# A mixture-of-experts stage of a two-block transformer: hidden activations turned on VectorE, slot tokens gathered with fp32r products, final rows fetched by indirect DMA

## The reference, cut to what matters

```python
logits = (hf @ router_w + router_b).astype(jnp.float32)
top_logit, top_idx = lax.top_k(logits, TOP_K)                 # TOP_K = 4, 256 tokens
gates = jax.nn.softmax(top_logit, axis=-1)
...
def expert_block(args):
    xb, e = args
    y = clamped_swiglu(xb @ w_gu[e] + b_gu[e])                # 1024 -> 2 * 1024, then 1024
    return y @ w_down[e] + b_down[e]
...
y_rows = y_rows * row_gate[:, None].astype(y_rows.dtype)
out = jax.ops.segment_sum(y_rows, row_tok, num_segments=n_tok + 1)[:n_tok]
...
x = x + g2 * moe_ffn(...)
return rmsnorm(x, final_g)
```

## Time and profile before

| | us |
|---|---|
| median of three runs | 3607.09 |
| lowest and highest of the runs | 3606.88, 3608.83 |
| the profiled execution, span of its instructions | 3608.5 |
| TensorE busy | 3112.7 (86%) |
| VectorE, ScalarE, GpSimd busy | 1452.6, 898.5, 298.1 |

### The profile page before, as it was taken

One profiled execution on the slowest core, in us unless ns is written; L12 is line 12 of the kernel. 1 busy time (PEld: TensorE's weight loads), 2 busy tenths in 40 slices (PEclk: granted clock), 3 DMA queues, 4 the chain that ended last, 5 costly groups with the idle time before them and its releaser, 6 DMA issues. The chain is left out here.

```text
span 3608.5 us, 95079 instructions
## 1 busy us (share of the span) xinstructions
PE 3112.7 (86%) x42406; PEld 2242.3 (62%) x42406; DVE 1452.6 (40%) x2335; ACT 898.5 (25%) x1523; POOL 298.1 (8%) x236
## 2 busy tenths in 40 slices
PE   5978879998887888787897976676999999999996
PEld 3855558887565676674786866543566566666653
DVE  3355653333763554556565765524111111111111
ACT  2114322222223343332343542201011000111100
POOL 0021200000411132230000104000000000000000
PEclk7989889999898999997998987887999999999998
DMA  7242432222143101003653430222999999999993
GB/s 288 82 158 77 155 140 85 101 96 93 38 155 123 50 21 38 34 4 125 233 187 121 166 115 3 101 102 94 399 404 406 408 407 405 406 405 406 409 405 139
DMA packets 220724, 684.11 MB, mean 190 GB/s; under 512 B 26096, under 2 KB 51184, under 8 KB 187712
## 3 DMA queue, kind: packets, MB, share of 16 engines
q1 hardware_dynamic: 190288, 647.72, 46.8%
q10 hardware_dynamic: 30192, 32.77, 2.7%
HBM read 659.46 MB, written 20.97 MB: 189 GB/s over the span
## 5 line engine op out<-in xcount | busy, mean ns | idle before, releaser
L3480 PE MATMUL experts_psum_gu<-ring,experts_x 128*32 128x256 f32 x9216 | 507.9, 381 | 16.6 <-ACT experts_x L3524 16.6
L3480 PEld LDWEIGHTS experts_psum_gu<-ring,experts_x 128*32 128x32 f32 x9216 | 295.6, 110 | 219.8 <-ACT experts_x L3524 16.9
L3584 DVE TENSOR_TENSOR experts_gate<-experts_psum_gu,experts_bias 128x768 f32<-128x768 f32 x32 | 30.6, 957 | 864.4 <-PE experts_psum_gu L3480 864.4
L3503 PE MATMUL experts_psum_down<-experts_weights,experts_hiddenT 128*32 128x256 f32 x6144 | 339.0, 380 | 4.3 <-ACT experts_hiddenT L3532 4.3
L3503 PEld LDWEIGHTS experts_psum_down<-experts_weights,experts_hiddenT 128*32 128x32 f32 x6144 | 199.5, 110 | 137.9 <-issue 6.3
L818 PE MATMUL mlp_psum_bank<-mlp_x_high,mlp_w_high 128*128 128x512 f32 (+1 forms) x512 | 174.8, 341 | 12.8 <-DVE xT_rounded L322 12.8
L3528 ACT ACTIVATE experts_sigmoid<-experts_gate 128x768 f32<-128x768 f32 x32 | 27.0, 843 | 615.5 <-DVE experts_gate L3586 615.5
L296 DVE TENSOR_TENSOR ring_rounded<-ring,mlp_w_high 128x1024 fp32r<-128x1024 f32 x128 | 156.7, 1225 | 51.3 <-ACT mlp_w_high L291 51.3
L818 PE MATMUL mlp_psum_bank<-xT_rounded,mlp_w_high 128*128 128x512 f32 (+1 forms) x512 | 175.4, 342 | 0.0
L818 PE MATMUL mlp_psum_bank<-mlp_x_high,ring_rounded 128*128 128x512 f32 (+1 forms) x512 | 173.6, 339 | 0.0
L3480 PE MATMUL experts_psum_gu<-xT,experts_x 128*32 128x256 f32 x3072 | 171.6, 379 | 0.0
(11 more groups left out here) (729 smaller groups left out, 5761.9 us busy)
## 6 DMA issues: line engine op xcount, KB each, us to landing
ring<-in_w_gu SPq DMA_DIRECT2D x186, 1024.0 KB, 18.9
experts_weights<-in_w_down SPq DMA_DIRECT2D x128, 1024.0 KB, 20.7
ring<-in_ada_w SPq DMA_DIRECT2D x36, 2048.0 KB, 9.0
ring<-in_mlp_w SPq DMA_DIRECT2D x32, 2048.0 KB, 7.9
xT<-in_w_gu SPq DMA_DIRECT2D x64, 1024.0 KB, 20.3
ring<-in_w_in SPq DMA_DIRECT2D x12, 2048.0 KB, 7.6
ring<-in_ab_w_in SPq DMA_DIRECT2D x6, 2048.0 KB, 9.1
ring<-in_w_rkv SPq DMA_DIRECT2D x6, 2048.0 KB, 8.4
```

Source lines behind the costliest of these rows:

```text
L3480: mm = nc.tensor.matmul(pg[o, q, gr, :], x, w[:, c:c + C], start=(u == 0 and gr != 1), stop=(u == U - 1), skip_group_check=True)
L3503: mm = nc.tensor.matmul(pd[o, gr, :], hidT[:, ch, gr, GROUP * v:GROUP * v + GROUP], w[:, ch, C * c:C * c + C], start=(v == 0 and ch == 0 a ...
L3584: v.tensor_tensor(gt[:, :, :], pg[:, 0, 0:GROUPS, :], rep(bias[:, 0, :], GROUPS), ALU.add).then_inc(s_bg, 1)
```

## The change

1. The loads of the router's weights and of the output biases move into norm2m's fetch.
2. In the router the tokens are split into a high part (rounded to fp32r) and a low part (the rest, rounded to fp32r; GpSimd subtracts). `S` is fp32r and lies in the memory of `acc`. The gather takes two single-pass products where one fp32 product stood, in groups of four PSUM banks: the half t = 0 of the group first, then t = 1. `s_S` is raised after each half of `S`. `gsel` is gone, and `rank` is copied to integers.
3. In the experts VectorE turns blocks of 32x32 of the hidden activations (`turned`) where TensorE and ScalarE turned blocks of 128x128; the rows of `w_down` are put in the order that this asks for. A wait for the last read of `gu` in PSUM (`s_bu`) goes ahead of `gate_up`.
4. In the last stage GpSimd fetches the four rows of each token by eight indirect DMAs of 128 rows (512 KB), and VectorE multiplies by the gates and sums. The table for the square root is loaded ahead, and the norm is done for each half apart.

```diff
@@ router @@
-        with nc.Block() as block:
-            @block.sync
-            def _(sync):
-                sync.dma_start(w[:, :, :], rw.rearrange("(a p) n -> p a n", p=P)).then_inc(s_ld, 16)
-                sync.dma_start(bd[:, :], bdown).then_inc(s_ld, 16)
...
-                pe.wait_ge(s_S, 1)
-                pe.wait_ge(s_tokc, 4)
-                for kt in range(KT):
-                    for sh in range(2):
-                        n = 2 * kt + sh
-                        if n >= 4:
-                            pe.wait_ge(s_xgc, n - 3)
-                        for t in range(2):
-                            mm = nc.tensor.matmul(pb[:, n % 4, :], htok[:, t, kt * P:(kt + 1) * P],
-                                                  S[:, t, sh * 512:(sh + 1) * 512], start=(t == 0), stop=(t == 1))
-                        mm.then_inc(s_xg, 1)
+                pe.wait_ge(s_high, 4)
+                pe.wait_ge(s_low, 4)
+                for first in range(0, 2 * KT, 4):
+                    for t in range(2):
+                        if first == 0:
+                            pe.wait_ge(s_S, t + 1)
+                        for n in range(first, first + 4):
+                            kt, sh = divmod(n, 2)
+                            if t == 0 and n >= 4:
+                                pe.wait_ge(s_xgc, n - 3)
+                            for q, h in enumerate((h_high, h_low)):
+                                mm = nc.tensor.matmul(pb[:, n % 4, :], h[:, t, kt * P:(kt + 1) * P],
+                                                      S[:, t, sh * 512:(sh + 1) * 512], start=(t + q == 0), stop=(t + q == 2))
+                            if t:
+                                mm.then_inc(s_xg, 1)
...
+                    nc.scalar.copy(h_high[:, n // 2, c], pb[:, n, :]).then_inc(s_high, 1)
+                    nc.scalar.copy(htok[:, n // 2, c], pb[:, n, :]).then_inc(s_tokc, 1)
...
+                    nc.gpsimd.tensor_tensor(h_low[:, n // 2, c], htok[:, n // 2, c], h_high[:, n // 2, c].bitcast(F32),
+                                            ALU.subtract).then_inc(s_low, 1)
@@ experts @@
                 def gate_up(i):
                     pe.wait_ge(s_x, i + 1)
+                    pe.wait_ge(s_bu, i + 1)
...
                 def down(i):
-                    pe.wait_ge(s_tc, i + 1)
+                    pe.wait_ge(s_t, i + 1)
                     pe.wait_ge(s_y, i + 1)
...
                 with pe.Fori(0, last) as i:
                     gate_up(i + 1)
                     down(i)
-                    turn_hidden(i + 1)
...
+                def turned():
+                    v.transpose(hidT[:, :, :, :].rearrange("p a b c -> p (a b c)"), up[:, :, :].rearrange("p a b -> p (a b)"))\
+                        .then_inc(s_t, 1)
+
+                v.sem_inc(s_bu, 1)
                 hidden(0)
+                turned()
                 with dve.Fori(0, last_item(dve)) as i:
                     hidden(i + 1)
+                    dve.wait_ge(s_dn_used, i * V + 2 * V)
+                    turned()
@@ final @@
+            @block.gpsimd
+            def _(pool):
+                for t in range(2):
+                    for k in range(TOP_K):
+                        nc.gpsimd.indirect_dma_start(yt[:, t, k, :], None, y_dram[0:N_PAIR, :],
+                                                     bass.IndirectOffsetOnAxis(rank_int[:, t, k:k + 1], 0))\
+                            .then_inc(s_yt[t][k], 16)
...
+                    for k in range(TOP_K):
+                        dve.wait_ge(s_yt[t][k], 16)
+                        ch.link(nc.vector.scalar_tensor_tensor(out=a, in0=yt[:, t, k, :], scalar=topg[:, t, k:k + 1], in1=a,
+                                                               op0=ALU.mult, op1=ALU.add))
                     ch.link(nc.vector.tensor_tensor(a, a, gate_row, ALU.mult))
                     nc.vector.tensor_tensor(g.x[:, 2 + t, :], g.x[:, 2 + t, :], a, ALU.add).then_inc(s_x, 1)
...
+                    if t:
+                        dve.wait_ge(s_row, 16)
+                        finish(dve, ch, 0)
+                finish(dve, ch, 1)
@@ the caller @@
             norm_T(g, "norm2m", LAT_TILES, g.xT, lambda t: mod(4, t), lambda t: mod(3, t), gains[:, 1, :], off=2,
-                   fetch=Fetch(g, "ldmoe", [(rb[:, :], row(a["router_b"])), (iota[:, :], row(a["iota"]))]))
+                   fetch=Fetch(g, "ldmoe", [(rb[:, :], row(a["router_b"])), (iota[:, :], row(a["iota"])),
+                                            (rw[:, :, :], a["router_w"].rearrange("(a p) n -> p a n", p=P)),
+                                            (bd[:, :], a["b_down"])]))
```

More of the change, by code:

```diff
@@ L3169, with router @@
 N_ITEM = N_EXP + (N_PAIR - 1) // (ITEM + 1) + 1
-def router(g, rw, rb, iota, bdown, acc, rank, topg, XgT, table, S, gsel):
+def router(g, w, rb, iota, bd, acc, rank, rank_int, topg, XgT, table, S):
     nc = g.nc
     with Phase(g, "router") as ph:
-        w = ph.sb("w", [P, KT, N_EXP])
-        bd = ph.sb("bd", [N_EXP, D])
         lg = ph.sb("logits", [P, 2, N_EXP])
@@ L3372, in _ @@
                     v.tensor_copy(gT[:, t, :], pl[0:N_EXP, t, 0:P]).then_inc(s_gc, 1)
-                for t in range(2):
-                    ch.link(v.tensor_scalar(gsel[:, t, :], iota, rank[:, t, 0:1], topg[:, t, 0:1],
-                                            ALU.is_equal, ALU.mult))
-                    for k in range(1, TOP_K):
-                        ch.link(v.tensor_scalar(g.tmp[:, :], iota, rank[:, t, k:k + 1], topg[:, t, k:k + 1],
-                                                ALU.is_equal, ALU.mult))
-                        ch.link(v.tensor_tensor(gsel[:, t, :], gsel[:, t, :], g.tmp[:, :], ALU.add))
                 ch.wait()
@@ L3409, in experts @@
         s_gt, s_up, s_pr, s_sg, s_h = (ph.sem(x) for x in ("gate", "up", "product", "sigmoid", "hidden"))
-        s_t, s_tc, s_y, s_st, s_end = (ph.sem(x) for x in ("turned", "turned_copied", "y", "stored", "end"))
+        s_t, s_y, s_st, s_end = (ph.sem(x) for x in ("turned", "y", "stored", "end"))
         def unit(u):
@@ L3566, in _ @@
                     result(i)
-                    turned(i + 1)
                 sigmoid(last)
                 result(last - 1)
-                turned(last)
                 result(last)
@@ L3896, in block2 @@
             norm_T(g, "norm2m", LAT_TILES, g.xT, lambda t: mod(4, t), lambda t: mod(3, t), gains[:, 1, :], off=2,
-                   fetch=Fetch(g, "ldmoe", [(rb[:, :], row(a["router_b"])), (iota[:, :], row(a["iota"]))]))
+                   fetch=Fetch(g, "ldmoe", [(rb[:, :], row(a["router_b"])), (iota[:, :], row(a["iota"])),
+                                            (rw[:, :, :], a["router_w"].rearrange("(a p) n -> p a n", p=P)),
+                                            (bd[:, :], a["b_down"])]))
             gate_rows(g, "rows3", [lambda kt: g.mods[0][:, 40 + kt, 0:1]], rows)
-            router(g, a["router_w"], rb[:, :], iota[:, :], a["b_down"], acc, rank[:, :, :], topg[:, :, :], XgT,
-                   table, acc, gsel)
+            router(g, rw, rb[:, :], iota[:, :], bd, acc, rank[:, :, :], rank_int[:, :, :], topg[:, :, :], XgT,
+                   table, slots)
         experts(g, a["w_gu"], a["w_down"], a["b_gu"], XgT, table, y_dram)
-        final(g, acc, gsel, y_dram, rows[:, 0, :], row(a["final_g"]), out)
+        final(g, acc, rank_int, topg, y_dram, rows[:, 0, :], row(a["final_g"]), out)
 def program(nc, a, out, parts=(0, 1, 2), x_out=None):
@@ L3958, in program, with hidden_order @@
         store(g, "stx", [(x_out[t], g.x[:, t, :]) for t in range(TT)])
+def hidden_order(w):
+    e, d, n = w.shape
+    return np.ascontiguousarray(w.reshape(e, 4, 8, 32, n).transpose(0, 2, 1, 3, 4).reshape(e, d, n))
 def layout(i):
```

117 lines of the change are left out of this document (43 added, 74 removed).

## The result

| | before | after |
|---|---|---|
| median of four runs, us | 3606.99 | 3552.04 |
| lowest and highest | 3606.74, 3608.83 | 3549.18, 3566.14 |
| span of the profiled execution | 3608.5 | 3547.6 |

The ratio is 0.9847, with an interval from 0.9829 to 0.9865: 1.5% faster. The predicted span was 3546.0 and the span is 3547.6. The runs of the changed kernel scatter over 17 us, so the sum is settled by the two traces, stage by stage. The stages are marked by the same four events in both: norm2m's first square on ScalarE, TensorE's first `gate_up`, the copy of the last rows but one, the copy of the last rows.

A forecast was written before the change was run, and what follows sets the result against it. The weight stream, 32.65 us an item, was taken to bound the expert loop. Gains of 29.1 (router) + 0 (loop) + 4.7 (last item) + 28.7 (last stage) = 62.5 us gave span 3546.0, median 3544.6; range 3537 to 3561.

The forecast's parts named there:

- Prefetch: Router's weights loaded in norm2m: 3.2 us removed at TensorE, 0.8 lost in VectorE's fetch wait; net gain 2.4 us.
- Gather: Router: from TensorE getting `S` to the last copy, 31.1 us before; split single-pass products gain 16.7 us.
- Rival B: Router's gather: the clock stays low for all 64 products, gain 5.4 us in place of 16.7, 3556 us; chance 0.06.
- `gsel`: Router's end: without it the copies into `acc` end the router, gain 10.0 us; the item table costs nothing yet.
- Loop: Experts: TensorE loses 1.2 us an item, but weight loads decide the end; gain 0 (bounds -1 and +1).
- rival C: Experts' loop does gain, the DMA rate not being at its limit: 36 us more, 3509 us; chance 0.04.
- Last item: Experts' end: copy and transpose side by side save 3.2 us, the clock staying up 1.5; gain 4.7 us.
- Last stage: Final norm with eight indirect gathers: ends 24.9 us after its start F, 53.6 before; gain 28.7 us (24 to 31).
- The step between gathers: Last stage: time from one indirect gather to the next, taken as 1.8 us, between bounds 1.3 and 4.1.
- Rival A: Last stage: gathers run one after another, 4.1 us each, gain 13 us in place of 28.7, 3560 us; chance 0.14.
- D: Whole kernel slower than before: GpSimd makes gather descriptors row by row, last landing at F + 80; chance 0.02.
- E: Last stage: VectorE is the bound, ending at F + 19.6 with gathers at 1.3 us; counted within the forecast.

The follow-up runs named there:

- no_fetch_wait: The changed kernel with VectorE's wait for the whole fetch in norm2m left out; median 3549.50 us, ratio 0.9821.
- r_after: The changed kernel once more, unedited; median 3556.04 us, ratio 0.9843 to the kernel before.
- after_again: The changed kernel unedited, run again beside other runs on the same chip; median 3555.01 us, ratio 0.9857.
- down0_first: The changed kernel with the first item's down weights loaded at the experts' start, ahead of item 1's gate-up; median 3550.86 us, ratio 0.9831.
- early2: The changed kernel without the fetch wait, with the first item's down weights first and two of its gate-up units loaded in the router; 3552.98 us (one run).
- half_after: The changed kernel loading only the first half of each gate-up unit's columns, 8 MB an item in place of 12; median 3530.43 us, ratio 0.9785.
- only_turn: The kernel before with only the vector transpose in the experts and its w_down layout; median 3609.49 us, ratio 0.9986.
- gathers_first: The changed kernel with VectorE starting its sums only when all eight gathers have landed; 3564.10 us (one run).
- best: The changed kernel without the fetch wait in norm2m and with the first item's down weights loaded at the experts' start; median 3549.48 us, ratio 0.9842.

## Why the prediction held, point by point

*Prefetch, +2.4 predicted, 0.9 measured.* The step that failed is VectorE's wait. I gave the two added loads 0.8 us between landing side by side and queueing; the wait grew by 1.90 us (1.54 to 3.44), more than either of my cases. Of 3.23 us won at TensorE's logits (I had 3.2), 1.90 and the 0.4 us that the products of rows3 took longer go off. no_fetch_wait shows that the whole 3.4 us of this wait are on the path: its logits begin 17.33 us after norm2m's first square, not 20.74.

*Gather, +16.7 predicted, 15.6 measured* (from the logits' start to the last slot copy, 57.67 to 42.07). The wait for the second half of `S` was as told (1.02 us, I had 1.2). The clock rose later than I had it: all eight products behind that wait ran at the lower clock, 3.46 us, where half of them and 2.6 us were forecast. The product was mis-sized: 0.233 us and not the 0.217 of the earlier trace rows, 0.8 us over the 48 at the full clock. More than half of that is a wrong reading of mine, not the chip: the 46 products of the earlier trace rows count those that lie across the window's ends, and the same products by their starts in the kernel before are (1896.92 - 1894.20) / 12 = 0.227 us apart:

```profile
1894.20 0.62 PE L832 MATMUL mlp_psum_bank<-mlp_w_high,mlp_hidden_high 128*128 128x512 f32 x2
...
1896.92 0.62 PE L832 MATMUL mlp_psum_bank<-mlp_w_high,mlp_hidden_high 128*128 128x512 f32 x2
```

Against these 1.6 us stand 0.6 us at the end: the last copies were through 0.9 us behind the last product, and I had 1.5. Rival B is out, since the 48 others ran at the full clock. The subtractions took 1.23 us each and were hidden.

*`gsel`, +10.0 predicted, 10.15 measured* (copy's end to first gate_up: 15.45 to 5.30). The item table ended at 2464.5, about level with the last slot copy (2465.5), as told. What the prediction left out is the clock behind the gather, which costs up to 2.7 us in some executions (r_after, after_again, down0_first and early2 had it). No experiment has the prefetch, the gather or `gsel` alone; these three gains are read from the two traces.

*Loop, 0 predicted, 0.5 measured*, within what the program differs from itself. This was the step on which 36 us hung, and each link has its run: TensorE's own period is 31.08 (half_after), where I had 30.8, since the turn was worth 0.94 us an item and not 1.2; the stream's is 32.5 to 32.6 whatever the order, the lead is used up after twelve items, and rival C is right only in a kernel with fewer bytes. The early loads add why it can't be bought back at the start.

*Last item, +4.7 predicted, 4.9 measured*, the clock at 2.4 GHz and a pause of 1.81 us. From ScalarE's copy of the rows to TensorE's next start it is 1.04 us and was 4.31, 3.3 us less (I had 3.2); the clock gives the other 1.6 (I had 1.5). only_turn has it alone, 4.9.

*Last stage, +28.7 predicted, 27.5 measured.* Mis-sized by 0.9 us is the first gather (F + 5.4, not 4.5), and VectorE's operations with two SBUF inputs took 1.31 us in the sum, not 1.25. The step between gathers, 1.8 us, is 2.1 and 2.0 us for the first three as VectorE uses them; the bytes of the last have moved by F + 16.1, so over all eight it is about 1.6 (an estimate, with the 0.7 us that gathers_first shows between the last bytes and their use). Rival A (4.1 us) is out, D too. But the path was not the one that I took: I let the last gather decide (F + 17, and F + 21 for `x`), and VectorE never waited for it. What ends the stage is VectorE, as in E, only with `x` at F + 22.3 where E had 19.6: 5.40 until the first gather, 15.38 of work, 1.53 of waits, 3.74 for the finish. Of the Trainium skill's page (DMA: Bandwidth & Descriptors, "Anatomy of one DMA — SWDGE (gpsimd) path") the estimate of 3.2 us is below the 4.6 us of the first gather here, and as a price of each in turn it is too high: in gathers_first eight took 15.1 us from the first issue to the last landing, not 25.6. The 4.6 us are not those of a gather alone on the DMA engines, since the 512 KB of `final_g`, issued at F, and the next gathers move beside it.

*The runs.* The median came out 7.4 us above the forecast one, the trace 1.6. Of the rest most is likely the part ahead of norm2m: of the 9.1 us between the spans of the changed kernel's trace and r_after's (3547.6, 3556.7), that part makes 9.3, from 2402.69 to 2411.99. The other runs have no trace. Where that spread comes from wasn't tried; the half loads only show that it isn't the weights of the experts.

## What to carry to other kernels

When an engine runs without a gap, look at whether its loads keep pace: a time from issue to landing that grows over the loop says that the engine lives on a lead, and a shorter loop body only uses it up sooner. Such a lead can't be longer than the buffers, so loading earlier is worth nothing once they fill in the first items; a third fewer bytes an item (8 MB in place of 12) would be worth 27 us here. An indirect gather that puts each row where it is wanted is cheap beside a product with a 0/1 matrix: the last stage took 26 us against 54, and both fetch 4 MB. And a count of operations in a window holds those that lie across its ends; a rate is safer from two starts.

## What the hardware showed that I had not expected

- An indirect DMA of 128 rows of 4 KB costs GpSimd 0.94 us of issue and 0.30 between two. Beside VectorE's sums single issues took up to 1.80 us in the changed kernel and up to 1.94 in best and after_again; in gathers_first, without them, none was over 0.94 but the first (1.15).
- Gathers overlap: the first is usable after 4.6 us, and eight in a row land some 1.5 us apart by the estimate from gathers_first, 0.52 MB each, 347 GB/s, where the loads that SyncE issues moved 395 to 412 in the experts.
- Behind the same pauses of TensorE (0.74 and 0.26 us) the granted clock fell to 1.2 GHz in four of ten traces and stayed at 2.4 in six, worth 2.7 us. A pause of 1.81 us ahead of the last item left it at 2.4. The length of the pause alone doesn't tell.
- An fp32r product of 512 columns came every 0.233 us in the gather, and every 0.227 in the feed-forward layer, both at a granted clock of 1.00. Why they differ wasn't tried.
